# Order of a second input projection, and attention preparation moved into the attention blocks

## What is computed

```python
def second_block(x, ...):
    h = rmsnorm(x, norm1_g[l])
    q, k, v, u = jnp.split(h @ w_in[l], splits, axis=-1)     # 512, 128, 128, 512 columns
    a = attention_mixer(q, k, v, q_norm_g[l], k_norm_g[l], ang_row, ang_col)
    p = pool_mixer(u, pool_w[l], pool_b[l], pool_scale[l])
    x = x + jnp.concatenate([a, p], axis=-1) @ w_out[l]
    ...
def attention_mixer(q, k, v, ...):       # 8 query heads, 2 key heads of 64, all 1024 keys
    q = axial_rope(rmsnorm(q, q_g), ang_row, ang_col)
    k = axial_rope(rmsnorm(k, k_g), ang_row, ang_col)
    # per block of 128 queries: softmax(q k^T / 8) v
def pool_mixer(u, ...):                  # 4 groups of 128 columns, windows 2, 4, 8, 16
    # mean over a window around each token, minus the token; times a 128x128 matrix
```

## Time and profile before

| what | value |
|---|---|
| median of 3 runs | 2560.7 us (2559.79 to 2563.22) |
| the profiled execution | 2565.24 us, span 2563.3 us |
| TensorE busy | 2409.8 us, 94% of the span |
| VectorE busy | 1266.6 us, 49% |
| ScalarE busy | 832.0 us, 32% |
| GpSimd busy | 339.0 us, 13% |
| mean granted clock of TensorE | 0.976 of full speed |

### The profile page before, as it was taken

How to read it: one execution, slowest core, us unless ns; L and a number is a source line. 1 busy time by engine, 2 the same in 40 slices (tenths; PEclk the granted TensorE clock), 3 DMA queues, 4 the chain that set the end, 5 groups by cost and what they waited for, 6 DMA issues and landing times. The chain is left out here.

```text
span 2563.3 us, 28634 instructions
## 1 busy us (share of the span) xinstructions
PE 2409.8 (94%) x10895; PEld 1944.7 (76%) x10895; DVE 1266.6 (49%) x1537; ACT 832.0 (32%) x1247; POOL 339.0 (13%) x259
## 2 busy tenths in 40 slices
PE   5999965899999999999998969999999999999998
PEld 4788864677788888888876737777788888888887
DVE  5467246636644444444447359994423333333333
ACT  4232134834422222222235347873321111111111
POOL 1120012413100000000013606651000000000000
PEclk8999987999999999999999989999999999999999
DMA  8146421132211111111123230003111111111111
GB/s 315 57 134 201 143 79 62 33 115 80 60 50 43 48 49 49 49 49 49 50 99 120 58 90 20 22 9 115 34 50 50 49 49 49 49 49 49 49 48 67
DMA packets 188860, 181.92 MB, mean 71 GB/s; under 512 B 8349, under 2 KB 166893, under 8 KB 188145
## 3 DMA queue, kind: packets, MB, share of 16 engines
q1 hardware_dynamic: 185648, 173.36, 21.3%
q0 software_dynamic: 2176, 7.36, 0.9%
q10 hardware_dynamic: 961, 0.18, 0.0%
HBM read 152.55 MB, written 28.33 MB: 71 GB/s over the span
## 5 line engine op out<-in xcount | busy, mean ns | idle before, releaser
L289 PE MATMUL ps<-hhi,whi 128*128 128x512 f32 x1760 | 690.8, 393 | 2.7 <-DVE wlo L215 2.0
L291 PE MATMUL ps<-hhi,wlo 128*128 128x512 f32 x1760 | 686.4, 390 | 0.0
L290 PE MATMUL ps<-hlo,whi 128*128 128x512 f32 x1760 | 686.3, 390 | 0.0
L215 DVE TENSOR_TENSOR wlo<-raw,whi 128x1024 fp32r<-128x1024 f32 x178 | 229.8, 1293 | 369.0 <-ACT whi L210 369.0
L289 PEld LDWEIGHTS ps<-hhi,whi 128*128 128x128 f32 x1760 | 331.5, 188 | 74.3 <-DVE wlo L215 2.4
L290 PEld LDWEIGHTS ps<-hlo,whi 128*128 128x128 f32 x1760 | 331.5, 188 | 70.5 <-issue 1.9
L291 PEld LDWEIGHTS ps<-hhi,wlo 128*128 128x128 f32 x1760 | 331.4, 188 | 69.3
L210 ACT ACTIVATE whi<-raw 128x1024 fp32r<-128x1024 f32 x178 | 184.5, 1049 | 388.0 <-PE ps L2246 286.8
L2397 DVE TENSOR_TENSOR arena<-arena,ps 128x1024 f32<-128x1024 f32 x160 | 195.2, 1220 | 141.1 <-PE ps L2246 140.2
L2244 PE MATMUL ps<-hid_hi,whi 128*128 128x512 f32 x640 | 250.0, 391 | 0.0
L2245 PE MATMUL ps<-hid_lo,whi 128*128 128x512 f32 x640 | 249.2, 389 | 0.0
(11 more groups left out here) (318 smaller groups left out, 3206.7 us busy)
## 6 DMA issues: line engine op xcount, KB each, us to landing
raw<-in_w_up SPq DMA_DIRECT2D x66, 512.0 KB, 3.7
raw<-in_w_down SPq DMA_DIRECT2D x44, 512.0 KB, 3.5
raw<-in_w_in SPq DMA_DIRECT2D x32, 512.0 KB, 5.0
arena<-in_w_ada SPq DMA_DIRECT2D x32, 512.0 KB, 4.7
raw<-in_w_gate SPq DMA_DIRECT2D x22, 512.0 KB, 3.7
raw<-in_w_out SPq DMA_DIRECT2D x16, 512.0 KB, 3.6
arena<-x_park SPq DMA_DIRECT2D x2, 4096.0 KB, 12.2
x_park<-arena SPq DMA_DIRECT2D x4, 2048.0 KB, 8.9
```

The lines of the kernel that those rows point to most:

```text
L215: nc.vector.tensor_tensor(wlo[:, w.off % RING, :], raw[:, w.off % RAW, :], whi[:, w.off % RING, :].bitcast(F32), ALU.subtract).then_inc(lo ...
L289: nc.tensor.matmul(acc[:, tok], whi[:, s, ws], hhi[:, k, tok], start=(k == 0), stop=False)
L290: nc.tensor.matmul(acc[:, tok], whi[:, s, ws], hlo[:, k, tok], start=False, stop=False)
L291: mm = nc.tensor.matmul(acc[:, tok], wlo[:, s, ws], hhi[:, k, tok], start=False, stop=(k == DK - 1))
```

## The change

The second input's tiles come in the order keys, values, pooled groups 1, 2, 3, queries 0 to 3, pooled group 0. From tile 6 on, TensorE works by channel groups (`product_by_tiles`) and issues the head chain's products of the tile before between them; the last tile also holds the value transposes, all into one PSUM buffer, and raises a semaphore `passed` by which ScalarE and VectorE write keys and values over the part of `hlo` that has been used. The root and the product with the sine are kept in PSUM. Queries 0 to 2 are stored behind the weight loads, query 3 during the attention's first units.

The blocks of preparation and attention become one for each attention: a lead object (`FirstLead`, `SecondInput`) gives each engine's program ahead of the attention, and, for the second, pieces at its first units: the rest of pooled group 0 on GpSimd, rope and low part of query 3 on VectorE, its high part on ScalarE. The pool products go into the first two tiles of the output projection, at channel groups 2 and 5. The values are copied and subtracted in one piece. Low key parts are multiplied over 64 partitions, without zeros; low probability parts (in the second attention) into 64 rows of output. The exponential's table set is no longer loaded for the second attention. The pool weights lie elsewhere.

```diff
             if o < T_OUT2:
-                return columns(a["w_in_2"], w + ((4 if o < T_IN2 + 6 else -6) - T_IN2))
+                r = o - T_IN2
+                return columns(a["w_in_2"], w + ((4 if r < 2 else 5 if r < 5 else -5 if r < 9 else -3) - T_IN2))
...
+        def product_by_tiles(pe, acc, w, between, passed=None):
+
+            s = w.off % RING
+            pe.wait_ge(lo_done, w.val(add=1 + RAW))
+            for k in range(DK):
+                if k in between:
+                    between[k]()
+                ws = slice(k * P, (k + 1) * P)
+                for h in range(2):
+                    o, tok = acc[:, half(h)], half(h)
+                    nc.tensor.matmul(o, whi[:, s, ws], hhi[:, k, tok], start=(k == 0), stop=False)
+                    nc.tensor.matmul(o, whi[:, s, ws], hlo[:, k, tok], start=False, stop=False)
+                    mm = nc.tensor.matmul(o, wlo[:, s, ws], hhi[:, k, tok], start=False, stop=(k == DK - 1))
+                if k == DK - 1:
+                    mm.then_inc(used, 1)
+                elif passed:
+                    mm.then_inc(passed, 1)
...
+                if k == 5 and after_five:
+                    after_five(pe)
...
-            vall = lflat[:, 0:vblocks * 384].rearrange("p (k g x) -> p k g x", g=2, x=192)
             kn = T + pad
-            o = vblocks * 384
-            khh = lflat[:, o:o + 2 * kn].rearrange("p (g t) -> p g t", g=2)
-            klo = lflat[:, o + 2 * kn:o + 4 * kn].rearrange("p (g t) -> p g t", g=2)
-            assert o + 4 * kn <= DK * T
-            qsts = [v.rearrange("p (j s t) -> p j s t", s=2, t=P) for v in (att_r[:, 0:1024], gflat)]
+            o = 4 * kn
+            khh = lflat[:, 0:2 * kn].rearrange("p (g t) -> p g t", g=2)
+            klo = lflat[:, 2 * kn:o].rearrange("p (g t) -> p g t", g=2)
+            vall = lflat[:, o:o + vblocks * 256].rearrange("p (k g x) -> p k g x", g=2, x=P)
+            assert o + vblocks * 256 <= DK * T
+            qsts = [v.rearrange("p (j s t) -> p j s t", s=2, t=P) for v in (gflat, att_r[:, 0:1024])]
...
+                def turned(self):
+                    return down[0][:, :].rearrange("p (c g d) -> p c g d", g=2, d=64)
 
                 def act_values(self, act):
-                    for c in range(NB):
-                        act.wait_ge(S["vturned"], c + 1)
-                        nc.scalar.activation(vall[:, c + pad // P, :, 64:128],
-                                             up[c % 2][:, 0:P].rearrange("p (g d) -> p g d", g=2),
-                                             ACT.Copy).then_inc(S["vhi"], 1)
-
-                def dve_keys(self, dve):
-                    nc.vector.memset(klo[64:128, :, :].bitcast(F32), 0.0)
-                    if not full:
-                        nc.vector.memset(klo[0:64, :, 0:P].bitcast(F32), 0.0)
-                        nc.vector.memset(khh[:, :, 0:P].bitcast(F32), 0.0)
-                        nc.vector.memset(vall[:, 0, :, 0:128].bitcast(F32), 0.0)
-                    nc.vector.memset(vall[:, :, :, 128:192].bitcast(F32), 0.0)
-                    dve.wait_ge(S["keys"], 4)
-                    for g in range(2):
-                        nc.vector.tensor_tensor(klo[0:64, g, pad:kn], ka[64 * g:64 * g + 64, :],
-                                                khh[64 * g:64 * g + 64, g, pad:kn].bitcast(F32), ALU.subtract)
+                    act.wait_ge(S["vturned"], 1)
+                    nc.scalar.activation(vall[:, pad // P:, :, 64:128], self.turned(), ACT.Copy).then_inc(S["vhi"], 1)
+
+                def dve_pads(self, dve):
+                    nc.vector.memset(klo[0:64, :, 0:P].bitcast(F32), 0.0)
+                    nc.vector.memset(khh[:, :, 0:P].bitcast(F32), 0.0)
+                    nc.vector.memset(vall[:, 0, :, :].bitcast(F32), 0.0)
+
+                def dve_keys(self, dve, g):
+                    dve.wait_ge(S["keys"], 2 * g + 2)
+                    nc.vector.tensor_tensor(klo[0:64, g, pad:kn], ka[64 * g:64 * g + 64, :],
+                                            khh[64 * g:64 * g + 64, g, pad:kn].bitcast(F32), ALU.subtract).then_inc(S["klo"], 1)
 
                 def dve_values(self, dve):
-                    for c in range(NB):
-                        dve.wait_ge(S["vhi"], c + 1)
-                        nc.vector.tensor_tensor(vall[:, c + pad // P, :, 0:64],
-                                                up[c % 2][:, 0:P].rearrange("p (g d) -> p g d", g=2),
-                                                vall[:, c + pad // P, :, 64:128].bitcast(F32),
-                                                ALU.subtract).then_inc(S["vlo"], 1)
...
                 def pe(self, pe):
                     for c in range(NB):
-                        if c >= 2:
-                            pe.wait_ge(S["vlo"], c - 1)
-                        nc.tensor.transpose(up[c % 2][:, 0:P], va[:, c * P:(c + 1) * P],
-                                            identF[:, :]).then_inc(S["vturned"], 1)
-
-            if stage is not None:
-                stage(Keys())
-            else:
-                with nc.Block(name + "_keys") as block:
-                    @block.scalar
-                    def _(act):
-                        keys = Keys()
-                        keys.act_keys(act)
-                        keys.act_values(act)
-
-                    @block.vector
-                    def _(dve):
-                        keys = Keys()
-                        keys.dve_keys(dve)
-                        keys.dve_values(dve)
-
-                    @block.tensor
-                    def _(pe):
-                        Keys().pe(pe)
-
-                    @block.gpsimd
-                    def _(pool):
-                        clear(pool, used_up)
+                        mm = nc.tensor.transpose(down[0][:, c * P:(c + 1) * P], va[:, c * P:(c + 1) * P], identF[:, :])
+                    mm.then_inc(S["vturned"], 1)
+
+            lead = stage(Keys())
...
+                        if n.off == 1:
+                            sp.wait_ge(S["scores"], 1)
                         for j in range(parts):
                             if full and n.off == 0 and n.i is None:
-                                sp.wait_ge(q_stored[j], 64)
+                                lead.sp_query(sp, j)
...
-                        nc.scalar.preload_act_table_set(EXP if full else LN_EXP)
+                        lead.act(act)
                         exponentials(At(0), 0)
 
                     def body(n, more):
                         for e in range(per_n):
+                            if full and n.off == 0 and n.i is None:
+                                lead.act_unit(act, e)
...
+                        lead.pool(pool)
                         if not full:
+                            pool.wait_ge(S["vlo"], 1)
...
-                                mm = nc.tensor.matmul(acc[:, ks], q[:, h // 2, h % 2, :], klo[:, g, ks], start=False,
+                                mm = nc.tensor.matmul(acc[:, ks], q[0:64, h // 2, h % 2, :], klo[0:64, g, ks], start=False,
...
-                                nc.tensor.matmul(o_, v[:, 0:128], pths[g][:, k, :], start=(k == 0), stop=False,
+                                nc.tensor.matmul(o_, v, pths[g][:, k, :], start=(k == 0), stop=False,
                                                  skip_group_check=True)
-                                mm = nc.tensor.matmul(o_, v[:, 64:192], ptls[g][:, k, :], start=False,
+                                mm = nc.tensor.matmul(o_[0:64, :], v[:, 64:128], ptls[g][:, k, :], start=False,
...
+                        lead.pe(pe)
+                        pe.wait_ge(S["klo"], 1 if full else 2)
                         scores(At(0), 0)
+                        lead.pe_second(pe)
                         scores(At(0), 1)
+                        pe.wait_ge(S["vlo"], 1)
 
                     def body(n, more):
                         for e in range(per_n):
+                            if full and n.off == 0 and n.i is None:
+                                if e == 2:
+                                    pe.wait_ge(S["klo"], 2)
+                                lead.pe_unit(pe, e)
...
+                        lead.dve(dve)
                         maxima(At(0), 0)
+                        lead.dve_second(dve)
                         maxima(At(0), 1)
...
+        ROPED2 = (0, 5, 6, 7, 8)
+        POOLED2 = (2, 3, 4, 9)
...
+                for t in range(4, N_IN2 + 4):
+                    load(sp, At(t + T_IN2), tile_source(At(t + T_IN2)))
+                    if t >= 11:
+                        self.store(sp, t - 11)
...
+            def sp_query(self, sp, j):
+
+                if j == 3:
+                    self.store(sp, j)
+                sp.wait_ge(q_stored[j], 64)
...
+                for t in range(4, N_IN2):
+                    pe.wait_ge(up_free, in2_base + t + 1)
+                    w, acc = At(t + T_IN2), up[t % 2]
+                    if t < 6:
```

(163 more changed lines are left out.)

332 lines of the change are left out of this document (121 added, 211 removed).

## The result

The changed kernel takes 2604.24 us (median of 4 runs, 2602.11 to 2606.19) against 2560.24 for the kernel before beside it: 1.0164 times as long, 95% interval 1.0151 to 1.0177. The profiled execution has a span of 2601.0 us and a mean clock of 0.975. The forecast was 2539; the kernel is 44 us slower instead of 21 faster.

A forecast was written before the change was run, and what follows sets the result against it. TensorE, busy 94% of the span, was taken as the bound, so time lay only in its waits and useless work. -29.4 + 9.7 + 1.5 + 6.9 - 10.0 = -21.3 us, from 2560.7 to 2539 us; range 2530 to 2560.

The forecast's parts named there:

- The narrower matmuls: Low key products over 64 rows, low probability products into 64 columns: no matmul shortened, shape changes taken to cost 0.
- the 0.093 from which the sum turns: Cost in us per row change in both attentions from which the forecast gain of 21.3 us is eaten.
- The upper bound that I had named (0.165): Upper bound in us per row change: the part of a 0.39 us matmul that runs on under its successor.
- the column case: First attention: a 128x128 product followed a 128x64 one after 0.23 us, so a column change loses nothing.
- the only row case I had (128 to 4): Four matmuls from 151.45 us, next start at 153.26: 0.09 us for the row change, with other possible causes.
- The drain rival: Both attentions: each row change drains TensorE, 0.165 us or more, 49 us in sum, 2588 us, slower; chance 0.12.
- The pool products: Moved from the hole into the first two output tiles, where TensorE is the full engine: +6.9 us.
- second input and hole, first score: Second input projection and the stretch behind it: second attention's first score at 1502.4 instead of 1531.8, -29.4 us.
- start of the second attention: First score to unit 6's maximum: 29.1 us against 19.4, +9.7, with query 3 late; +1.5 for possible lower clock.
- first attention, first score: Query fetch issued at the attention's start, first score at 420.4: -10.7 us.
- first attention, to the projection behind it: First attention in all: first score -10.7 us, value split between two maxima +0.7, together -10.0 us.
- The two stalls forecast for tiles 6 and 9: Second input projection: late norm of query 0 in tile 6, +1.7 us; root behind key copies in tile 9, +0.3.

The follow-up runs named there:

- with 128 rows: Changed kernel, but the low key products of both attentions take 128 rows again, unused rows zeroed by GpSimd: 2552.75 us, 0.9967 of the kernel before.
- with 64 rows: Changed kernel, 64 rows kept, residual x fetched for the second output projection in three transfers instead of one: 2594.55 us, 1.0129 of the kernel before.
- both misses mended: Changed kernel with 128-row low key products in both attentions and residual x in three transfers, run in two groups: 2541.45 and 2542.12 us.
- the first one with x in parts: First run group of the changed kernel with 128-row low key products and residual x in three transfers: 2541.45 us, 0.9913 of the kernel before.
- the fourth query's experiment: Changed kernel with 128 rows and x in three transfers, plus query 3's low part split in unit 2 instead of 3: 2546.2 us, repeated 2541.95.

## Why the prediction was wrong

**The step that failed is "The narrower matmuls", where I took 0 for a change of rows.** It is 0.15 to 0.17 us a change on the mean in the second attention, above the 0.093 from which the sum turns. The upper bound that I had named (0.165) was none: a single change costs up to 0.20. I chose 0 because the column case showed 0; but rows and columns are different cases, and the only row case I had (128 to 4) showed 0.09, which is what the first part of a change costs; behind it stood 32 tiny transposes in one merged row, in which the second part may have lain unseen. The drain rival had the mechanism and nearly the price: it gave 49 us (28 in the second attention, 21 in the first), the runs 51.5 (32 and 19.4). That this comes so close is in part luck, because its reading of TensorE's own work was low: a head in the kernel before takes TensorE 2.78 us (1601.92 to 1604.70), 22.2 a block and not 21.8, so 1.4 us were to spare and not 1.8. The rule of the Trainium skill, TensorEngine Tiling (Array Packing), Key Properties, that a change of the tiling mode drains TensorE, agrees with the trace for rows and not for columns (0.23 us between starts, and 1.0003 in time).

**A second step was missed altogether.** Under "The pool products" I counted their own time only: 6.9 us, right (the pair lasts 30.55 us, from 1707.78 to 1738.33, in the profile with 128 rows, and 23.6 before). But the last operand's split also releases SyncE's transfer of x, 12.1 us long, which had just fitted before. Its price is 9.7 us with 64 rows and 10.6 to 11.3 with 128, all between kernels of two groups (9, and 10 to 14, by the ratios). No rival held it.

**The other steps, by the profiles.**

| step | forecast | measured |
|---|---|---|
| second input and hole, first score | -29.4 | -31.3, with 128 rows and in the changed kernel |
| start of the second attention | +9.7 and +1.5 | +12.3 with 128 rows (the whole attention, 211.6 less 199.3) |
| pool products | +6.9 | +7.0 |
| first attention, first score | -10.7 | -10.8 |
| first attention, to the projection behind it | -10.0 | -11.1 with 128 rows (509.06 to 497.93); 9.0 of it are left at the second input |
| changes of columns | 0 | 0 |
| changes of rows | 0 | +51.5 |
| late residual | not seen | +9.7 |

With 128 rows the -31.3 is the shift of the second attention's first score (1531.84 to 1491.55, 40.3 us) less the 9.0 us by which the second input begins earlier (1396.85 against 1405.82). The two stalls forecast for tiles 6 and 9 (+1.7 and +0.3) did not appear: TensorE was busy for all of the 74.6 us that hold these tiles, and these 2.0 us are about the difference from -29.4. The fourth query was late in the way worked out, its fetch issued 26.1 us after the first score (25.8 forecast), with TensorE waiting 4.8 us for it. Forecast and misses add up: 2539 + 51.5 + 9.7 = 2600, and 2604.2 was measured; the other 4 us stay unexplained. With both misses mended, 2541.5 and 2542.1 were measured. The chance of 0.12 on the drain was too low for a price with an open bound on the losing side and 384 places at which it is paid.

## What to carry to other kernels

In these runs contracting over half the rows saved no time on a stream of 512 columns (a 64-row product takes 0.39 us where the shape stays, as one with 128 rows does), and it cost about 0.17 us at each change to or from 128 rows; zero the unused rows and keep the shape, or group the products by shape. When work moves into a stage, look for every transfer that waits for that stage's last operand: one that used to land just in time is the next stall. A price that the trace does not show, multiplied by hundreds of places, deserves a measurement or an even chance, not the kinder of its two bounds.

## What the runs showed of the hardware

- A change of the weights' columns (128 to 64 and back, 128 rows) leaves 0.23 us between starts, with the weights loaded one product ahead. A change of rows leaves 0.32 to 0.43 us, and the load is not ahead.
- The direction of the change makes no difference that shows; what stood ahead does. A change behind a product that itself followed without one costs 0.09 us, a change behind a product that brought one costs 0.19 to 0.20, to 64 rows and back alike. With 512 columns streamed these are the 0.32 and 0.43 us above. With 256 columns, in the first attention of the changed kernel, the first step into 64 rows leaves 0.21 us, and the step back and the next step into 64 rows 0.31 each; with 128 rows starts are 0.12 apart.

```profile
435.17 0.28 PE L1730 MATMUL ps<-hlo,query_operand 128*128 128x256 f32 x1
435.38 0.38 PE L1732 MATMUL ps<-hlo,query_operand 64*128 64x256 f32 x1
435.69 0.39 PE L1730 MATMUL ps<-hlo,query_operand 128*128 128x256 f32 x1
436.00 0.38 PE L1732 MATMUL ps<-hlo,query_operand 64*128 64x256 f32 x1
```

- The granted clock dips in some executions at 140 to 160 us, far ahead of every edit: 0.89 to 0.93 in six of the twelve profiles (the kernel before and the one with 128 rows among them), 1.00 in the other six (the changed kernel and the first one with x in parts among them). Where it dips, the first attention's stage starts at 412.5 to 416.4 us, where it does not, at 409 to 411. The first pair of the fourth query's experiment fell on the two sides: 0.92 and 415.8 with the edit, 1.00 and 410.1 without, and these are the 5.8 us that its profile lost ahead of the edit.
